# Norm totals in two rounded matmuls instead of one fp32 matmul, masks ahead of the scores, and 256 columns in the last mixer

## The chip, the cores and the metric

One core of one Trainium2 chip runs the whole program. The metric is device time in microseconds (us); the median of three runs before the change is 1474.05 us. TensorE does the matmuls, ScalarE the activations and copies that round, VectorE the elementwise work, GpSimd a share of it, and SyncE issues the loads.

## The reference

Two models run one after the other on 16 + 256 = 272 tokens of width 1024: a block with retention and forgetting attention, and then two layers, each of which is

```python
h = h + 0.5 * swiglu(rmsnorm(h, ffn1_norm[l]), ...)
h = h + hybrid_mixer_2(rmsnorm(h, mix_norm[l]), ...)
h = h + 0.5 * swiglu(rmsnorm(h, ffn2_norm[l]), ...)
# hybrid_mixer_2
q, k, v, a, b, g_sb, g_conv = split(u @ w_in)
y_sb = stick_breaking_attention(q, k, v) @ w_attn_out
y_conv = silu(layernorm(depthwise_conv31(a * sigmoid(b)))) @ w_conv_out
m = (sigmoid(g_sb) * y_sb + sigmoid(g_conv) * y_conv) @ w_out
```

Every norm divides by a root of a mean over the 1024 channels (512 in the layer norm), computed for each token. The channels lie on the partitions, so a sum over channels is a matmul with a matrix of ones. Only the last 256 tokens are returned.

## The kernel before

Activations are kept transposed: 128 channels on the partitions, tokens along the free dimension. A "slab" is a weight matrix of 1024 x 128 (eight 128 x 128 blocks); for each block TensorE runs three fp32r matmuls (high weight by high activation, high by low, low by high: lines 1509 to 1511 in `slab`, 1570 to 1572 in `first_pair`), 24 in all, into one of four PSUM banks `W[0..3]`. SyncE loads a slab to `raw`, ScalarE rounds it (`hi`, line 475), VectorE or GpSimd subtracts the rounded part (`lo_ahead`, line 904; `lo`, line 417). Each engine runs its own list of instructions in order; semaphores tie them. The weights of a slab go into one of four slots, and `hi_ahead` for the slab three places on stands in ScalarE's list at step `s` of the current one. TensorE may start slab `s` only when slab `s` - 3 has been taken out of its bank (`emptied`, `evac_done`).

**Norm statistics.** The squares of the 8 chunks of `h` are added into `acc` by VectorE (line 930). `stat(p)` is one fp32 matmul of `ones` by `acc`, placed inside `first_pair` (the first two slabs of the next stage, interleaved block by block) ahead of block `STAT_AT` = 5. ScalarE takes the root (line 483) and VectorE the reciprocal (line 910), which scales every slab of the stage as it leaves its bank (`scaled`, line 915). There are such totals for norms p = 1 to 7, and one more (`fin_acc`) of the first block's final norm, directly behind `first_pair` of the first layer.

**The mixer** runs 36 slabs, steps s = 0 to 35 of `for s in range(4 * N_MIX)`, on every engine. With `SB_FROM` = 14, `c, phase = divmod(s - 14, 4)`: TensorE runs `scores(c)` behind the slab of phase 0 (c = 0 to 3), `values(c - 1)` behind that of phase 1 (c = 1 to 4), `sums(c)` behind that of phase 3. ScalarE and VectorE do the softening between (`soften`, `keeps`, `round_keep`, `weights`). VectorE also runs the 31 taps of four channel groups (`taps`, line 1364) in those steps, up to s = 29. `LN_FROM` = 30: at s = 30 VectorE adds the four groups (`ln_sum`), TensorE sums over channels in fp32 behind slab 31 (`channel_sums(1)`), VectorE subtracts the mean at s = 32, ScalarE squares at s = 33, VectorE adds at s = 34, TensorE sums behind slab 35 (`channel_sums(2)`), then root, reciprocal, gain, Silu and rounding, while TensorE runs four double slabs of the attention branch; the convolution branch waits for `s_lo`.

In the second layer the first 16 tokens aren't needed past the keys and values; the query, gate and output slabs run on 256 columns there (`t` = 16), but the convolution, the layer norm and the attention's output still run on 272.

## Time and profile before

| what | value |
|---|---|
| median of 3 runs | 1474.05 us (1473.8 to 1474.22) |
| profiled execution | 1474.35 us, its span 1472.5 us |
| PE busy | 1465.1 us, 99% |
| DVE, ACT, POOL busy | 903.1, 769.0, 495.6 us |
| granted TensorE clock, mean | 0.999 |
| chain that ended last | PE 97%, POOL 1%, DVE 1% |
| DMA | mean 170 GB/s |

A share of busy time counts a matmul from its start to its modelled end, so matmuls in a row overlap; what a matmul costs in a row is the distance between two starts. An fp32 matmul is recorded as two instructions.

### The profile page before, as it was taken

To read this page: it belongs to the slowest core of one execution; us is meant where nothing else is said; L and a number is where in the kernel's file an instruction comes from. 1 tells how busy PE (TensorE), PEld (TensorE's weight loads), DVE (VectorE), ACT (ScalarE), POOL (GpSimd) and SP (SyncE) were. 2 spreads that over 40 slices of the span, in tenths; PEclk is the share of its full clock that TensorE was granted. 3 is DMA by queue.
4 is the path that set the end of the run, shared out by engine and by line. 5 is a ranking of instruction groups with operands and counts; after the bars stand their busy time and mean duration, and the time that the engine had idled before them with its cause. 6 is when DMAs were issued, how large, how long until landed. Compare 5 with 4: busy or idle time off the path is not lost.

```text
span 1472.5 us, 31298 instructions
## 1 busy us (share of the span) xinstructions
PE 1465.1 (99%) x11531; PEld 1430.3 (97%) x11531; DVE 903.1 (61%) x1568; ACT 769.0 (52%) x1087; POOL 495.6 (34%) x208
## 2 busy tenths in 40 slices
PE   9999999999999999999999999999999999999998
PEld 7999999989999999999999999999999999999987
DVE  6437888755445468998644434444437899854443
ACT  6446655545444446567544544444435557654443
POOL 5541000443334304710244433433420660044443
PEclk9999999999999999999999999999999999999999
DMA  7335566655556545445555654555644545566663
GB/s 265 120 100 168 171 189 192 216 162 161 174 176 210 164 129 164 146 146 164 173 174 177 201 182 134 173 176 187 200 149 139 163 142 171 165 195 185 207 201 107
DMA packets 65852, 250.97 MB, mean 170 GB/s; under 512 B 7280, under 2 KB 8688, under 8 KB 65776
## 3 DMA queue, kind: packets, MB, share of 16 engines
q1 hardware_dynamic: 65776, 249.92, 54.7%
q8 instruction: 53, 0.87, 0.2%
q14 instruction: 23, 0.19, 0.0%
HBM read 248.84 MB, written 1.05 MB: 170 GB/s over the span
## 4 chain that ended last, share of the span: by engine, by line
PE 97%; POOL 1%; DVE 1%; DMA 0%; issue 0%; ACT 0%; SPq 0%; DVEq 0%; POOLq 0%
PE W L1509 27%; PE W L1511 27%; PE W L1510 27%; PE W L1604 5%; PE XP L1629 3%; PE W L1603 3%; PE XQ L1629 2%; PE W L1570 1%; PE W L1571 1%; PE W L1572 1%; DMA raw<-in_w 0%; POOL wlo L417 0%; PE XQ L1549 0%; PE XQ L1728 0%; ACT whi L475 0%
## 5 line engine op out<-in xcount | busy, mean ns | idle before, releaser
L417 POOL TENSOR_TENSOR wlo<-raw,whi 128x1024 fp32r<-128x1024 f32 (+1 forms) x183 | 476.1, 2606 | 939.8 <-ACT whi L475 939.8
L1509 PE MATMUL W<-xh,whi 128*128 128x272 f32 (+2 forms) x2400 | 691.2, 288 | 0.2 <-POOL wlo L417 0.2
L1511 PE MATMUL W<-xh,wlo 128*128 128x272 f32 (+2 forms) x2400 | 686.7, 286 | 0.0
L1510 PE MATMUL W<-xl,whi 128*128 128x272 f32 (+2 forms) x2400 | 685.3, 286 | 0.0
L475 ACT ACTIVATE whi<-raw 128x1024 fp32r<-128x1024 f32 (+1 forms) x437 | 483.3, 1110 | 129.8 <-PE W L1511 101.6
L1509 PEld LDWEIGHTS W<-xh,whi 128*128 128x128 f32 x2400 | 452.1, 188 | 3.0 <-issue 1.9
L1511 PEld LDWEIGHTS W<-xh,wlo 128*128 128x128 f32 x2400 | 452.2, 188 | 0.0
L1510 PEld LDWEIGHTS W<-xl,whi 128*128 128x128 f32 x2400 | 451.9, 188 | 0.3
L904 DVE TENSOR_TENSOR wlo<-raw,whi 128x1024 fp32r<-128x1024 f32 (+1 forms) x253 | 330.9, 1308 | 60.2 <-ACT whi L475 60.0
L1509 PE MATMUL W<-ax,whi 128*128 128x272 f32 (+2 forms) x838 | 241.0, 288 | 0.1
L1511 PE MATMUL W<-ax,wlo 128*128 128x272 f32 (+2 forms) x838 | 240.5, 287 | 0.0
L1510 PE MATMUL W<-ax,whi 128*128 128x272 f32 (+2 forms) x838 | 240.4, 287 | 0.0
L1510 PEld LDWEIGHTS W<-ax,whi 128*128 128x128 f32 x838 | 158.9, 190 | 0.1
L1509 PEld LDWEIGHTS W<-ax,whi 128*128 128x128 f32 x838 | 157.6, 188 | 0.6 <-DVE ax L1446 0.3
L1511 PEld LDWEIGHTS W<-ax,wlo 128*128 128x128 f32 x838 | 157.5, 188 | 0.0
L915 DVE TENSOR_TENSOR scr<-W,rinv 128x272 f32<-128x272 f32 (+2 forms) x140 | 60.4, 431 | 117.8 <-PE W L1511 117.1
L518 ACT ACTIVATE ax<-W 128x272 f32 (+3 forms) x88 | 34.7, 395 | 182.8 <-DVE W L993 182.8
L1604 PE MATMUL W<-ax,whi 128*128 128x512 f32 x330 | 115.6, 395 | 0.0
L515 ACT ACTIVATE scr<-scr 128x272 f32<-128x272 f32 (+1 forms) x110 | 46.9, 426 | 107.0 <-DVE scr L915 75.7
L915 DVE TENSOR_TENSOR W<-W,rinv 128x272 f32<-128x272 f32 (+1 forms) x88 | 39.1, 444 | 96.1 <-PE W L1511 96.1
L1364 DVE SCALAR_TENSOR_TENSOR XQ<-scr,prm,XQ 128x272 f32<-128x272 f32 x184 | 92.9, 505 | 5.7
L1603 PE MATMUL W<-ax,wlo 128*128 128x256 f32 x330 | 92.4, 280 | 0.0
(262 smaller groups left out, 1221.5 us busy)
## 6 DMA issues: line engine op xcount, KB each, us to landing
raw<-in_w SPq DMA_DIRECT2D x358, 512.0 KB, 3.6
raw<-in_w SPq DMA_DIRECT2D x80, 704.0 KB, 4.1
h<-in_hT SPq DMA_DIRECT2D x4, 272.0 KB, 4.9
scr<-in_cst SPq DMA_DIRECT2D x1, 1000.0 KB, 9.8
out<-h SPq DMA_DIRECT2D x3, 256.0 KB, 2.4
raw<-in_w SPq DMA_DIRECT2D x2, 256.0 KB, 3.7
cst<-in_cst SPq DMA_DIRECT2D x1, 472.0 KB, 7.7
out<-h SPq DMA_DIRECT2D x2, 128.0 KB, 2.2
```

The costliest lines, as they stand in the source:

```text
L417: pool.tensor_tensor(wlo[:, j, 0:cols], raw[:, j, 0:cols], whi[:, j, 0:cols].bitcast(F32), ALU.subtract).then_inc(lo_ready[j], 1)
L475: act.activation(whi[:, j, 0:cols], raw[:, j, 0:cols], ACT.Copy).then_inc(hi_ready[j], 1)
L515: act.activation(actv[:, b, t:], gate[:, b, 2 + t:T + 2], ACT.Silu).then_inc(act_ready, 1)
L904: dve.tensor_tensor(wlo[:, slot, 0:cols], raw[:, slot, 0:cols], whi[:, slot, 0:cols].bitcast(F32), ALU.subtract).then_inc(lo_ready[slot], 1)
L915: return dve.tensor_tensor(out, W[bank][:, t:T], rinv[:, t:], ALU.mult)
L1364: ins = dve.scalar_tensor_tensor(total, u[:, c, k:k + T], w, total, ALU.mult, ALU.add)
L1509: pe.matmul(out, whi[:, j, w], mh, start=start and k == 0, stop=False, skip_group_check=True)
L1510: pe.matmul(out, whi[:, j, w], ml, start=False, stop=False, skip_group_check=True)
L1511: ins = pe.matmul(out, wlo[:, j, w], mh, start=False, stop=stop and k == len(rhs) - 1, skip_group_check=True)
L1603: pe.matmul(W[out][:, 0:T - T_B], wlo[:, j, w], ah[:, c, T_B:], start=c == 0, stop=False, skip_group_check=True)
L1604: ins = pe.matmul(both, whi[:, j, w], ax[:, c, :, T_B:], start=False, stop=c == FC - 1, skip_group_check=True)
L1629: return pe.matmul(out, lhsT, rhs, start=start, stop=True, skip_group_check=True)
```

## The change

1. `round_sum` (ScalarE) copies `acc` to `sum_r[:, 0]` in fp32r, `low_sum` (VectorE) subtracts that from `acc` into `sum_r[:, 1]`, and `stat` becomes two fp32r matmuls with `minus_r` (minus ones); the sign goes into the `scale` of the root. `stat` moves from ahead of block 5 to behind the whole first pair. The statistic of p = 0 and that of the last norm stay as they are.
2. The total of the final norm of the first block goes the same way, and moves behind slab 2 of its stage.
3. Both channel totals of each mixer go the same way. The rounding stands in ScalarE's list at s = 31 and s = 35 ahead of `hi_ahead`, the subtraction in VectorE's list at s = 31 and s = 35 ahead of the evacuation of that slab.
4. In `scores` the two mask matmuls (fp32r) go ahead of the twelve score matmuls; `values(c - 1)` moves from behind the slab of phase 1 to behind that of phase 0, directly behind `scores(c)`.
5. In the second layer the taps, the layer norm, its Silu and rounding, and the attention's values run on 256 columns.

```diff
+        sum_r = ax[:, FC - 1, :, :]
@@ ScalarE
             def sqrt_stat(p, t=0, fin=False):
                 act.wait_ge(stat_mm, p + 1)
-                act.activation(rinv[:, t:], X[3][:, t:T], ACT.Sqrt, scale=1.0 / D,
+                act.activation(rinv[:, t:], X[3][:, t:T], ACT.Sqrt, scale=-1.0 / D if p else 1.0 / D,
+            def round_sum(p, t=0, fin=False):
+                act.wait_ge(acc_done, 8 * p + 8)
+                if fin:
+                    act.wait_ge(meta_sum, 1)
+                act.activation(sum_r[:, 0, t:], acc[:, t:], ACT.Copy).then_inc(sum_hi, 1)
@@ ffn_up
+                round_sum(p, ta, fin)
                 hi_ahead(g, 0, own, own)
                 sqrt_stat(p, ta, fin)
+                if fin:
+                    act.wait_ge(fin_add, DC)
+                    act.activation(sum_r[:, 0, T_B:], fin_acc[:, T_B:], ACT.Copy).then_inc(fin_hi, 1)
@@ mixer
-                            act.activation(u[:, k, CONV_K - 1:], y[:, k, :], ACT.Square).then_inc(ln_sq, 1)
+                            act.activation(u[:, k, CONV_K - 1 + t:], y[:, k, t:], ACT.Square).then_inc(ln_sq, 1)
+                    if s == 0:
+                        round_sum(p - 1)
+                    if s in (LN_FROM + 1, LN_FROM + 5):
+                        k = s // (LN_FROM + 5) + 1
+                        act.wait_ge(ln_sum, 2 * l + k)
+                        act.activation(sum_r[:, 0, t:], acc[:, t:], ACT.Copy).then_inc(ln_high, 1)
                     hi_ahead(g + s // 4, s % 4, K8A, K8A)
@@ VectorE
+            def low_sum(p, t=0):
+                dve.wait_ge(sum_hi, p)
+                dve.tensor_tensor(sum_r[:, 1, t:], acc[:, t:], sum_r[:, 0, t:].bitcast(F32), ALU.subtract).then_inc(sum_lo, 1)
@@ ffn_up
+                low_sum(p, ta)
                 lo_ahead(g, 0, own, own)
                 norm_factor(p, ta)
+                if fin:
+                    dve.wait_ge(fin_hi, 1)
+                    dve.tensor_tensor(sum_r[:, 1, T_B:], fin_acc[:, T_B:], sum_r[:, 0, T_B:].bitcast(F32), ALU.subtract).then_inc(fin_lo, 1)
@@ mixer
+                    if s in (LN_FROM + 1, LN_FROM + 5):
+                        k = s // (LN_FROM + 5) + 1
+                        dve.wait_ge(ln_high, 2 * l + k)
+                        dve.tensor_tensor(sum_r[:, 1, t:], acc[:, t:], sum_r[:, 0, t:].bitcast(F32),
+                                          ALU.subtract).then_inc(ln_low, 1)
@@ TensorE
             def stat(p, t=0):
+                if p:
+                    if p == 1:
+                        pe.wait_ge(minus_ready, 1)
+                    pe.wait_ge(sum_lo, p)
+                    mm(X[3][:, t:T], minus_r[:, :], sum_r[:, 0, t:], True)
+                    mm(X[3][:, t:T], minus_r[:, :], sum_r[:, 1, t:], False).then_inc(stat_mm, 1)
+                    return
@@ first_pair
-                    if k == STAT_AT and norm is not None:
-                        stat(norm, t[0])
...
+                if norm is not None:
+                    stat(norm, t[0])
@@ scores
+                    for bank in range(2):
+                        own = X[bank][:, 0:SBW].rearrange("p (s n) -> p s n", n=SB_SEG)[:, 0:3:2, :]
+                        masks = hider[:, :].rearrange("p (s n) -> p s n", n=SB_SEG)[:, 0:3:2, :]
+                        mm(own, identr[:, :], masks, True)
@@ values
+                        skip = 0 if b else t
...
-                            ins = mm(X[2][p0:p0 + 64, P * b:T], vT[:, b, P * c + p0:P * c + p0 + 64],
-                                     attn[:, bank, SB_AT[b]:SB_AT[b] + T - P * b], b == 0)
+                            ins = mm(X[2][p0:p0 + 64, P * b + skip:T], vT[:, b, P * c + p0:P * c + p0 + 64],
+                                     attn[:, bank, SB_AT[b] + skip:SB_AT[b] + T - P * b], b == 0)
@@ channel_sums
-                    pe.wait_ge(ln_sum, 2 * l + k)
-                    mm(X[3][:, 0:T], ones, acc[:, :], True).then_inc(ln_mm, 1)
+                    pe.wait_ge(ln_low, 2 * l + k)
+                    mm(X[3][:, t:T], minus_r[:, :], sum_r[:, 0, t:], True)
+                    mm(X[3][:, t:T], minus_r[:, :], sum_r[:, 1, t:], False).then_inc(ln_mm, 1)
@@ mixer
-                    if phase == 1 and 1 <= c <= CC:
+                    if phase == 0 and 1 <= c <= CC:
                         values(c - 1)
```

## Rows read from the trace of the kernel before

**Rows 1.** The page's busy times of each engine.

```profile
PE 1465.1 (99%) x11531; PEld 1430.3 (97%) x11531; DVE 903.1 (61%) x1568; ACT 769.0 (52%) x1087; POOL 495.6 (34%) x208
```

**Rows 2.** Timeline of PE around `stat(3)`: start, length, instruction, count.

```profile
531.67 0.62 PE L1549 MATMUL XQ<-acc,cst 128*128 128x272 f32 x2
...
532.25 0.29 PE L1571 MATMUL W<-xl,whi 128*128 128x272 f32 x1
532.38 0.29 PE L1572 MATMUL W<-xh,wlo 128*128 128x272 f32 x1
```

**Rows 3.** Timeline of PE around `scores(0)` of the first layer.

```profile
575.15 0.29 PE L1511 MATMUL W<-xh,wlo 128*128 128x272 f32 x1
575.37 1.10 PE L1629 MATMUL XP<-proj,scr 64*128 64x272 f32 x12
...
576.77 0.29 PE L1509 MATMUL W<-xh,whi 128*128 128x272 f32 x1
```

**Rows 4.** Timeline of PE around `values(0)` of the first layer.

```profile
594.93 0.29 PE L1511 MATMUL W<-xh,wlo 128*128 128x272 f32 x1
595.15 1.00 PE L1629 MATMUL XQ<-scr,vT 128*64 128x272 f32 x12
...
596.31 0.29 PE L1510 MATMUL W<-xl,whi 128*128 128x272 f32 x1
```

**Rows 5.** Timeline of PE at the channel totals (first layer once, then second).

```profile
643.73 0.73 PE L1629 MATMUL XQ<-acc,cst 128*128 128x272 f32 x2
...
1209.40 0.94 PE L1629 MATMUL XP<-ax,later_r 128*128 128x432 f32 x4
...
1216.84 1.00 PE L1629 MATMUL XQ<-scr,vT 128*64 128x272 f32 x12
1217.88 0.72 PE L1629 MATMUL XQ<-acc,cst 128*128 128x272 f32 x2
...
1218.56 0.28 PE L1510 MATMUL W<-xl,whi 128*128 128x256 f32 x1
...
1229.77 0.62 PE L1629 MATMUL XQ<-acc,cst 128*128 128x272 f32 x2
...
1230.35 0.28 PE L1510 MATMUL W<-ax,whi 128*128 128x256 f32 x1
```

**Rows 6.** Timeline of DVE, first layer: evacuations of slabs 27, 28, 29 and 31.

```profile
628.02 0.44 DVE L915 TENSOR_TENSOR proj<-W,rinv 128x272 f32<-128x272 f32 x1
...
632.16 0.44 DVE L915 TENSOR_TENSOR proj<-W,rinv 128x272 f32<-128x272 f32 x1 [0.16 <-PE W L1511]
...
635.19 0.44 DVE L915 TENSOR_TENSOR proj<-W,rinv 128x272 f32<-128x272 f32 x1 [0.20 <-PE W L1511]
...
644.69 0.43 DVE L915 TENSOR_TENSOR proj<-W,rinv 128x272 f32<-128x272 f32 x1
```

**Rows 7.** Timeline of DVE, second layer: evacuations of slabs 27, 29 and 31.

```profile
1203.17 0.42 DVE L915 TENSOR_TENSOR proj<-W,rinv 128x256 f32<-128x256 f32 x1
...
1209.76 0.41 DVE L915 TENSOR_TENSOR proj<-W,rinv 128x256 f32<-128x256 f32 x1
...
1219.21 0.42 DVE L915 TENSOR_TENSOR proj<-W,rinv 128x256 f32<-128x256 f32 x1
```

**Rows 8.** Windows: PE, PEld, DVE, ACT, POOL busy, clock, DMA share, GB/s.

```profile
1214.17:1224.07 9.90, 9.86 (x86) 9.38 (x85) 9.65 (x20) 9.21 (x11) 0.00 (x0) 1.00 0.37 115
1224.71:1228.69 3.98, 3.98 (x36) 3.98 (x35) 3.92 (x7) 1.76 (x2) 0.00 (x0) 1.00 0.72 208
...
1469.00:1470.00 1.00, 0.00 (x0) 0.00 (x0) 0.48 (x2) 0.00 (x0) 0.00 (x0) 1.00 1.06 352
```

**Rows 9.** Timelines of ACT and DVE behind `stat(7)`, entry of the last FFN.

```profile
1282.66 2.01 ACT L475 ACTIVATE whi<-raw 128x1024 fp32r<-128x1024 f32 x2 [1.36 <-PE W L1572]
...
1287.21 0.41 DVE L915 TENSOR_TENSOR scr<-W,rinv 128x256 f32<-128x256 f32 x1
```

**Rows 10.** Timeline of PE at the start of the program: `keep_warm`.

```profile
1.46 4.00 PE L1629 MATMUL XP<-vT 128*128 128x272 f32 x8 [1.46 <-DVE vT L1137]
```

More of the change, by code:

```diff
@@ L297, in build @@
         wo_half, minus_ready = sem("wo_half"), sem("minus_ready")
+        sum_hi, sum_lo, fin_hi, fin_lo = (sem(x) for x in ("sum_hi", "sum_lo", "fin_hi", "fin_lo"))
+        ln_high, ln_low = sem("ln_high"), sem("ln_low")
         glu_sig, u_ready, conv_step = (sem(x) for x in ("glu_sig", "u_ready", "conv_step"))
@@ L816, in out_hi @@
                     act.wait_ge(o_mm, CC * l + c + 1)
-                    act.activation(ah[:, c, :], X[2][:, 0:T], ACT.Copy).then_inc(o_hi, 1)
+                    act.activation(ah[:, c, t:], X[2][:, t:T], ACT.Copy).then_inc(o_hi, 1)
                 ga = g + N_MIX
@@ L865, in mixer @@
                     act.wait_ge(ln_silu, CC * l + c + 1)
-                    act.activation(ah[:, CC + c, :], y[:, c, :], ACT.Copy).then_inc(s_hi, 1)
+                    act.activation(ah[:, CC + c, t:], y[:, c, t:], ACT.Copy).then_inc(s_hi, 1)
                 hi_ahead(ga, 3, K8D, K8D)
@@ L1344, in taps @@
                     for c, k, in_psum, before in TAPS[s]:
-                        total = X[3][:, 0:T]
+                        total = X[3][:, t:T]
                         if k is not None:
@@ L1357, in taps @@
                         if k is None:
-                            ins = dve.tensor_tensor(y[:, c, :], total, y[:, c, :], ALU.add)
+                            ins = dve.tensor_tensor(y[:, c, t:], total, y[:, c, t:], ALU.add)
                         elif not in_psum:
-                            ins = dve.scalar_tensor_tensor(y[:, c, :], u[:, c, k:k + T], w, y[:, c, :], ALU.mult, ALU.add)
+                            ins = dve.scalar_tensor_tensor(y[:, c, t:], u[:, c, k + t:k + T], w, y[:, c, t:], ALU.mult, ALU.add)
                         elif k == EARLY_TAPS + 1:
-                            ins = dve.tensor_scalar(total, u[:, c, k:k + T], w, None, ALU.mult)
+                            ins = dve.tensor_scalar(total, u[:, c, k + t:k + T], w, None, ALU.mult)
                         else:
-                            ins = dve.scalar_tensor_tensor(total, u[:, c, k:k + T], w, total, ALU.mult, ALU.add)
+                            ins = dve.scalar_tensor_tensor(total, u[:, c, k + t:k + T], w, total, ALU.mult, ALU.add)
                         ins.then_inc(conv_step, 1)
@@ L1383, in mixer @@
                         dve.wait_ge(conv_step, TAP_N * (l + 1))
-                        dve.tensor_tensor(acc[:, :], y[:, 0, :], y[:, 1, :], ALU.add).then_inc(ln_step, 1)
-                        dve.tensor_tensor(sq[:, 0, :], y[:, 2, :], y[:, 3, :], ALU.add).then_inc(ln_step, 1)
+                        dve.tensor_tensor(acc[:, t:], y[:, 0, t:], y[:, 1, t:], ALU.add).then_inc(ln_step, 1)
+                        dve.tensor_tensor(sq[:, 0, t:], y[:, 2, t:], y[:, 3, t:], ALU.add).then_inc(ln_step, 1)
@@ L1386, in mixer @@
                         dve.wait_ge(ln_step, 5 * l + 2)
-                        dve.tensor_tensor(acc[:, :], acc[:, :], sq[:, 0, :], ALU.add).then_inc(ln_sum, 1)
+                        dve.tensor_tensor(acc[:, t:], acc[:, t:], sq[:, 0, t:], ALU.add).then_inc(ln_sum, 1)
+                    if s in (LN_FROM + 1, LN_FROM + 5):
[3 more added lines that the diff above has]
+                                          ALU.subtract).then_inc(ln_low, 1)
@@ L1398, in mixer @@
                         dve.wait_ge(ln_step, 5 * l + 5)
-                        dve.tensor_tensor(acc[:, :], acc[:, :], sq[:, 0, :], ALU.add).then_inc(ln_sum, 1)
+                        dve.tensor_tensor(acc[:, t:], acc[:, t:], sq[:, 0, t:], ALU.add).then_inc(ln_sum, 1)
                     if s < G_GLU:
@@ L1434, in mixer @@
                 dve.wait_ge(ln_sqrt, l + 1)
-                dve.reciprocal(sq[:, 0, :], acc[:, :]).then_inc(ln_rcp, 1)
+                dve.reciprocal(sq[:, 0, t:], acc[:, t:]).then_inc(ln_rcp, 1)
                 attn_gate(0)
@@ L1438, in mixer @@
                 for c in range(CC):
[L1439 removed]
+                    dve.tensor_tensor(y[:, c, t:], y[:, c, t:], sq[:, 0, t:], ALU.mult).then_inc(ln_norm, 1)
                 lo_ahead(ga, 1, K8D, K8D)
@@ L1473, in layer @@
                 ffn_down(g + L_DNA, p, K8D, 0.5, fin=l == 0)
+                low_sum(p)
                 lo_ahead(g + L_MIX, 0, K8D, K8D)
@@ L1581, in ffn_up @@
                 if fin:
-                    pe.wait_ge(fin_add, DC)
-                    mm(X[2][:, T_B:T], ones, fin_acc[:, T_B:], True).then_inc(fin_mm, 1)
-                for j in range(2, 4):
+                    project(g, 2, x_rhs(ta), t=ta)
+                    pe.wait_ge(fin_lo, 1)
+                    mm(X[2][:, T_B:T], minus_r[:, :], sum_r[:, 0, T_B:], True)
+                    mm(X[2][:, T_B:T], minus_r[:, :], sum_r[:, 1, T_B:], False).then_inc(fin_mm, 1)
+                for j in range(3 if fin else 2, 4):
                     t = tb if j % 2 else ta
@@ L1885, in scores @@
                             p0 = 64 * bank
-                            mm(X[bank][:, SB_AT[b]:SB_AT[b] + w], kpad[p0:p0 + 64, c, a:a + P], proj[p0:p0 + 64, QQ + c, a:T], b == 0)
-                    for bank in range(2):
-                        own = X[bank][:, 0:SBW].rearrange("p (s n) -> p s n", n=SB_SEG)[:, 0:3:2, :]
-                        masks = hider[:, :].rearrange("p (s n) -> p s n", n=SB_SEG)[:, 0:3:2, :]
-                        ins = mm(own, identr[:, :], masks, False)
+                            ins = mm(X[bank][:, SB_AT[b]:SB_AT[b] + w], kpad[p0:p0 + 64, c, a:a + P], proj[p0:p0 + 64, QQ + c, a:T], False)
                     ins.then_inc(z_mm, 1)
```

22 lines of the change are left out of this document (10 added, 12 removed).

## The prediction

> **What bounds the kernel now.** I read four views in this order. The page's busy times first: TensorE is busy 1465.1 us of a span of 1472.5 us, VectorE 903.1, ScalarE 769.0 [rows 1]. So the time is the length of TensorE's own list; a change pays only if it shortens that list, and costs only if it makes TensorE wait. Second the timeline of TensorE, read by distances between starts, because busy lengths overlap. Third the timelines of VectorE and ScalarE at the same places, to see what TensorE would wait for. Last the windows, for the sum of a chain of operations. The reader is to see that around the edit the mixer is tight: VectorE idles 0.16 and 0.20 us in the 7.17 us from slab 27 to slab 29 of the first layer and nowhere else up to slab 31 [rows 6], and not at all in the second layer [rows 7].
>
> Two lengths serve throughout. A slab on 272 columns takes 3.03 us (the evacuations of slabs 28 and 29, both right behind TensorE, are 632.16 and 635.19 [rows 6]). A slab on 256 takes 2.83: from 1218.56 less one matmul of 0.12 to 1229.77 there are four [rows 5].
>
> **What TensorE's list saves.**
>
> *Norm totals.* `stat(3)` starts at 531.67; the second fp32r matmul behind it starts at 532.25 and the third at 532.38, so one such matmul is 0.13 and the fp32 total costs 532.25 - 531.67 - 0.13 = 0.45 [rows 2]. Two rounded ones cost 0.25. Saved 0.20, for p = 1 to 7 and the total of the final norm: 8 x 0.20 = 1.6. Adding a wait there costs TensorE nothing: `stat` now stands 18 matmuls (2.3 us) later, and what it waits for (a copy of about 0.4 and a subtraction of about 0.4, as every 272-column operation of VectorE in rows 6) starts with the last addition, which was complete before the old place.
>
> The Trainium skill ("FP8 and Floating Point Precision", TensorE Precision Notes) has true fp32 as four passes of the array. By four times 0.13 the total would be 0.52 and the saving 0.27 each, 0.5 more in all for the eight; the row has 0.45, and the sum goes by it.
>
> *Channel totals.* Alone, the one at 1229.77 costs 1230.35 - 1229.77 - 0.12 = 0.46 [rows 5], against 0.25 or 0.24: 0.22 each, 0.9 for four. In the second layer TensorE also stood 1217.88 - 1216.84 - 0.93 = 0.11 before the first one; that goes into the new wait below. Sum 1.0.
>
> *Masks first, values behind scores.* A step between kinds costs time. Going into the scores TensorE starts at 575.37, where the next fp32r matmul would have started at 575.15 + 0.13 = 575.28: 0.09. Scores and masks end at 576.77, so the pair costs 1.49 [rows 3]. `values` goes in with the same 0.09 and out with 0.10: 596.31 - 0.13 - 595.06 = 1.12 in all, of which 0.93 is work [rows 4]. Together 2.61. In the new order: masks 0.27, in 0.09, scores 1.03, values 0.93, out 0.10 = 2.42. Saved 0.19 for each group that has both, c = 1 to 3 in two layers: 6 x 0.19 = 1.1. The bounds are 0 (if going from 64-row tiles of the scores to 64-column tiles costs as much as a change of kind) and 1.1; I take 1.1, since the rows show the cost at changes between fp32 and fp32r. Masks first by itself saves nothing: the work is the same and the step out only moves.
>
> *256 columns* on TensorE touch one of three blocks of `values`, 16 columns of 432 in 0.93: 0.03 x 4 = 0.1. Elsewhere they shorten VectorE.
>
> Total saved: 1.6 + 1.0 + 1.1 + 0.1 = 3.8 us.
>
> **What the new waits cost.**
>
> *First channel total, first layer.* Before, it waited for `ln_sum` alone, and TensorE got there at 643.73 [rows 5] with the sum just ready. Now there is a copy on ScalarE and a subtraction on VectorE, and the subtraction stands in VectorE's list behind the evacuation of slab 30 and its low part: exactly where the evacuation of slab 31 started, 644.69 [rows 6]. It ends 0.43 later, TensorE starts about 0.05 behind that: 645.17. TensorE itself would arrive at 643.83 (0.10 for the step out of fp32, which the old total didn't pay here). That is 1.34 if VectorE runs as before. It doesn't: `values` no longer lies between slabs 27 and 28, so TensorE does slabs 28 and 29 in 6.06, while VectorE's work between the evacuations of slabs 27 and 29 is 7.17 - 0.16 - 0.20 = 6.81 [rows 6]. VectorE starts at slab 27's end in both orders (its list over a whole group is about 15.8 of 16.2 us), so it is now 0.75 late at slab 29, and all that follows up to the sum is a fixed list. Wait: 1.34 + 0.75 = 2.1 us.
>
> *The same, second layer.* TensorE from slab 29's end, 1209.40, arrives before at 1216.84 + 0.93 = 1217.77, so 8.37 later [rows 5], and 8.44 in the new order. VectorE between slabs 27 and 29 has 6.59 [rows 7], less nine shorter operations at 16 columns less (0.017 each, the 0.43 against 0.41 of rows 6 and 7) = 6.42, against 5.66 of TensorE: with the 0.2 from a slab's end to its evacuation it stands at 0.96 behind slab 29's end. From there to the subtraction 1219.21 - 1209.76 = 9.45 [rows 7], less 13 x 0.017 = 9.23, then 0.41 and 0.05: 10.65. Wait 10.65 - 8.44 = 2.2.
>
> What is late next: in ScalarE's list at s = 31 the rounding waits for the same sum ahead of `hi_ahead`. The high part of slab 34 and all behind it (table load, high part, `out_hi`, the sigmoid of eight gates, table load, squares, high part of slab 36) slide by 3.6 us. From the start of the first to the end of the last that list is 9.21 busy in the old trace [rows 8]. It starts behind the copy, 1.4 ahead of the total, so the high part of slab 36 is ready 7.8 to 7.9 behind the start of the total, its low part on VectorE 1.2 later; TensorE wants it after four slabs, 11.6 and more. Hidden. The load into that slot waits for the low part, not for the later high part, and slides by under 2 us of a 12 us turn. VectorE, however, has that low part ahead of the additions of the squares, and then three additions, an evacuation and another low part: 3.92 busy together [rows 8], then the subtraction, 0.4. That puts the second rounded total 7.9 + 3.9 + 0.4 + 0.05 = 12.3 behind the start of the first. TensorE arrives 0.25 + 4 x 3.03 = 12.4 behind in the first layer: no wait. In the second, 0.24 + 11.33 = 11.57 against 12.3 less shorter operations 0.3 = 12.0: 0.4. Waits at channel totals: 2.1 + 2.2 + 0.4 = 4.7.
>
> *Entry of each FFN.* The root now starts behind the pair and delays two high parts (2.01) that started at 1282.66, by 0.55 [rows 9]: 0.2 to 0.3 from the matmul to the root, 0.47 the root. VectorE's low part and the first evacuation, 1287.21, follow: done at 1288.17. TensorE wants the bank two slabs and two rounded matmuls behind the pair; the old pair ended 0.1 behind 1282.66, the new one 0.45 sooner: 1282.32 + 0.24 + 5.66 = 1288.22. It fits with 0.05 to spare in the last FFN and with 0.3 to 0.4 in those on 272 columns, where slabs are longer. I take 0.1 for the lot, with bounds 0 and 1.5. In the mixer's entry the root stood behind a high part that starts at the pair's end anyway, so the move doesn't lengthen it.
>
> Sum: -3.8 + 4.7 + 0.1 = **+1.0 us**. The profiled execution took 1474.35 us (span 1472.5, 1.85 around it), so its like would be 1475.35; the median of the runs is 0.3 below that execution, so **1475.0 us**.
>
> **The rivals.**
>
> A, *the forecast*: TensorE's list is shorter by about 3.8 and the totals wait about as much. Bounds: 1472.5 (VectorE isn't pushed by the move of `values`, -1.5, and the second total doesn't wait, and a little more saved) to 1477.3 (nothing saved by the merge, 1.1, and 1.2 at the FFN entries).
>
> B, *the waits are hidden*: 1474.05 - 3.8 = 1470.2. For it speaks that VectorE and ScalarE have 39% and 48% of the span free; against it the order of VectorE's list behind `ln_sum`, 1.8 us that nothing shortens.
>
> C, *other side, the FFN entries*: the first evacuation misses TensorE at four entries. Price 1 us each where POOL's and VectorE's low parts collide: 1475.0 + 4 = 1479. It decides from a root more than 0.4 later than I have it, on 272 columns. Against it: everything in that chain is in rows 9 with its length.
>
> D, *the clock*: a wait of 2.2 us lets TensorE fall from its level of 2.4 GHz to 1.2. At the program's start eight passes took 4.00, 0.50 each [rows 10], where two passes of a total later take 0.45 together [rows 2]; one slab at that rate is 3 us more. One such slab per layer: 1475.0 + 6 = 1481. Against it: with no matmul for some 3 us at the end of the program the granted clock still reads 1.00 in 1469 to 1470 [rows 8]. The Trainium skill ("TensorE: Matmul & The Clock Gate", Why this matters for your kernels) warns of gaps in the middle of a kernel that bring the clock back to half; by that rule waits of 2 us are near enough to count this case, and the row speaks for the full clock.
>
> E, *the change of type doesn't pay*: two rounded matmuls cost what one fp32 did. Then 12 x 0.2 = 2.4 is missing: 1477.4. Rows 2 speak against it.
>
> **How the numbers follow.** A 0.73, B 0.13, C 0.06, D 0.04, E 0.04. A measurement of this kernel can tell 0.2% (2.95 us) from no change: 1471.1 to 1477.0. Faster is B and a sliver of A, 0.14. Slower is C, D, E and 0.04 of A: 0.18. The same: 0.68. The likeliest case alone has 1472.5 to 1477.3; toward B the range reaches to 1471.3, toward C to 1477.6, which leaves out most of B, C and D, 2 in 10.
>
> **What the new profile would show.** Right: the total at s = 31 starts 10 to 11 us behind slab 29's end in both layers, with TensorE idle about 2 us before it, and ScalarE's high part of slab 34 directly behind the new copy. `stat` behind the first pair without idle time. `values` directly behind `scores`, the step between them under 0.05. The second total waits in the second layer only. PE busy less by about 4 us and its idle time more by 5. Wrong: if the idle before the totals is under 1 us, B; if TensorE waits for evacuation behind the third slab of an FFN, C; if matmuls behind the wait are 0.24 apart, D.

## The result, and the profile after

The changed kernel takes 1478.13 us (median of 10 runs, 1476.81 to 1479.79), the one before 1474.20 (10 runs, 1473.80 to 1474.41): ratio 1.0025, interval 1.0017 to 1.0033. It is slower by a quarter of a per cent, clear of the noise of both. The forecast was 1475.0 us, with 1477.6 as its upper end.

The profiled execution took 1476.81 us with a span of 1475.0, against a span of 1472.5 before: +2.5 us, where the sum of the prediction had +1.0. The median of the runs lies another 1.3 us above that execution; this second part has its own cause (the clock, below).

The page of the changed kernel, busy times of the engines and the chain that ended last:

```profile
PE 1461.2 (99%) x11531; PEld 1428.5 (97%) x11531; DVE 906.1 (61%) x1580; ACT 772.6 (52%) x1099; POOL 494.9 (34%) x208
...
PE 95%; DVE 3%; POOL 1%; DMA 0%; ACT 0%; issue 0%; SPq 0%; DVEq 0%; POOLq 0%
```

TensorE has the same number of matmuls and is busy 3.9 us less than in [rows 1], and the kernel is slower all the same: of the chain 3% is VectorE now. TensorE's longest waits in the changed kernel (instruction line, who released it, us in total, times, longest); two shorter ones, of 0.4 and 0.3 us, lie before 24 us:

```profile
PE XQ L1671 <- DVE ax L1420: 3.8, 2, 2.1
PE XQ L1671 <- DVE ax L1032: 1.5, 1, 1.5
PE XP L1671 <- DVE vT L1166: 1.5, 1, 1.5
PE W L1544 <- DVE wlo L924: 0.5, 1, 0.5
```

The third is the start of the program ([rows 10]), there before too. L1420 is the subtraction of the channel totals, L1032 that of the final norm's total, L924 a low part of weights.

TensorE's timeline, at the final norm's total, the first channel total of each layer and the second one of the second layer (the bracket is the idle time before the instruction):

```profile
333.99 0.41 PE L1671 MATMUL XQ<-ax,minus_r 128*128 128x272 f32 x2
334.23 0.29 PE L1544 MATMUL W<-xh,whi 128*128 128x272 f32 x1
...
337.13 0.29 PE L1546 MATMUL W<-xh,wlo 128*128 128x272 f32 x1
338.95 0.50 PE L1671 MATMUL XQ<-ax,minus_r 128*128 128x256 f32 x2 [1.53 <-DVE ax L1032]
...
644.47 0.29 PE L1546 MATMUL W<-xh,wlo 128*128 128x272 f32 x1
646.52 0.52 PE L1671 MATMUL XQ<-ax,minus_r 128*128 128x272 f32 x2 [1.76 <-DVE ax L1420]
646.88 0.28 PE L1544 MATMUL W<-xh,whi 128*128 128x272 f32 x1
...
1218.51 0.28 PE L1546 MATMUL W<-xh,wlo 128*128 128x256 f32 x1
1220.87 0.50 PE L1671 MATMUL XQ<-ax,minus_r 128*128 128x256 f32 x2 [2.08 <-DVE ax L1420]
1221.21 0.28 PE L1544 MATMUL W<-xh,whi 128*128 128x256 f32 x1
...
1232.45 0.28 PE L1546 MATMUL W<-xh,wlo 128*128 128x256 f32 x1
1232.71 0.50 PE L1671 MATMUL XQ<-ax,minus_r 128*128 128x256 f32 x2
```

Read by distances between starts, with 0.13 (0.12 on 256 columns) for the matmul before: the totals start 1.69, 1.92, 2.24 and 0.14 late. A pair that TensorE reaches in its stride costs 334.23 - 333.99 = 0.24; behind a wait, 1221.21 - 1220.87 = 0.34. Each wait costs 0.1 more than it lasts.

From one total to the next the whole difference can be placed. The starts of the norm totals of the changed kernel are taken back by the 18 matmuls that now stand ahead of them (2.15, 2.26 or 2.12 us on 258, 272 or 256 columns):

| stretch | before | after | difference | what it is made of |
|---|---|---|---|---|
| start to `stat(1)` | 143.68 | 143.61 | -0.1 | nothing |
| to `stat(2)` | 187.65 | 188.12 | +0.5 | low part 0.5 late and a restart, less one total |
| to `stat(3)` | 200.34 | 201.71 | +1.4 | final norm's total 1.69 late, restart 0.1, less two totals |
| to first channel total, first layer | 112.06 | 113.08 | +1.0 | 1.92 late, less one total and three merges |
| to the second | 12.67 | 12.46 | -0.2 | one total |
| to `stat(4)` | 52.44 | 52.29 | -0.2 | one total |
| `stat(4)` to `stat(6)` | 399.81 | 399.39 | -0.4 | two totals |
| to first channel total, second layer | 109.23 | 110.21 | +1.0 | 2.24 late instead of 0.11, less one total and three merges |
| to the second | 11.89 | 11.84 | 0.0 | 0.14 late, restart, less one total |
| to `stat(7)` | 50.43 | 50.08 | -0.4 | restart, less one total |
| to TensorE's last group | 185.99 | 185.86 | -0.1 | one total |

The sum is +2.5. A "restart" is the 0.1 us behind a late start, a "merge" the joining of `scores` and `values`.

Rows for the merge of `values` with `scores`, which answer to [rows 3, 4]:

```profile
591.75 0.29 PE L1546 MATMUL W<-xh,wlo 128*128 128x272 f32 x1
591.88 0.42 PE L1671 MATMUL XP<-hider,identr 128*128 128x288 f32 x2
592.23 1.10 PE L1671 MATMUL XP<-proj,scr 64*128 64x272 f32 x12
593.26 1.00 PE L1671 MATMUL XQ<-scr,vT 128*64 128x272 f32 x12
594.19 0.40 PE L1544 MATMUL W<-xh,whi 128*128 128x272 f32 x1
594.42 0.29 PE L1545 MATMUL W<-xl,whi 128*128 128x272 f32 x1
```

The three together cost 594.42 - 591.75 - 0.25 = 2.42, as forecast (2.61 before). From scores to values there is no step: 593.26 - 592.23 = 1.03, and in the kernel before the masks start just as long behind the scores (575.37 and 576.40).

Why the final norm's total was late: the timelines of DVE and POOL there.

```profile
334.95 1.85 DVE L930 RECIPROCAL rinv<-rinv 128x272 f32<-128x272 f32 x1 [1.98 <-ACT rinv L486]
336.72 2.18 DVE L1032 TENSOR_TENSOR ax<-scr,ax 128x256 fp32r<-128x256 f32 x1
...
336.25 2.37 POOL L420 TENSOR_TENSOR wlo<-raw,whi 128x1024 fp32r<-128x1024 f32 x1 [8.32 <-ACT whi L478]
```

The subtraction L1032 has 256 columns and should take 0.4. It took 2.18 and ended 0.3 behind GpSimd's low part (336.25 + 2.37 = 338.62), beside which it ran. That it also stands behind a reciprocal of 1.85 was in the code, but I had costed only its own length. Alone at that place it would have ended at 336.72 + 0.42 = 337.14, before TensorE was there (337.13 + 0.13 = 337.26): what made TensorE wait is the time beside GpSimd. The kernel before had the same thing at the same place, in a low part of VectorE, where it cost nothing (DVE, then POOL):

```profile
335.97 2.58 DVE L904 TENSOR_TENSOR wlo<-raw,whi 128x1024 fp32r<-128x1024 f32 x1 [1.61 <-ACT whi L475]
...
335.07 2.39 POOL L417 TENSOR_TENSOR wlo<-raw,whi 128x1024 fp32r<-128x1024 f32 x1 [7.55 <-ACT whi L475]
```

Alone that low part takes 1.21, as the next one in the changed kernel does:

```profile
338.82 1.21 DVE L924 TENSOR_TENSOR wlo<-raw,whi 128x1024 fp32r<-128x1024 f32 x1
```

### The profile page after: what moved, and what is told of

Same layout as the page of the kernel before. It is cut to its first block, busy times and chain, and to the rows that moved or that the text cites. A ratio compares the mean times of both kernels' runs of the same rounds, so it can differ in the third digit from the quotient of the medians.

```text
span 1475.0 us, 31325 instructions
## 1 busy us (share of the span) xinstructions
PE 1461.2 (99%) x11531; PEld 1428.5 (97%) x11531; DVE 906.1 (61%) x1580; ACT 772.6 (52%) x1099; POOL 494.9 (34%) x208
## 4 chain that ended last, share of the span: by engine, by line
PE 95%; DVE 3%; POOL 1%; DMA 0%; ACT 0%; issue 0%; SPq 0%; DVEq 0%; POOLq 0%
PE W L1544 26%; PE W L1545 26%; PE W L1546 26%; PE W L1646 5%; PE W L1645 3%; PE XP L1671 2%; PE XQ L1671 2%; PE W L1608 1%; PE W L1609 1%; DVE XQ L1393 1%; PE W L1610 1%; DMA raw<-in_w 0%; DVE wlo L924 0%; POOL wlo L420 0%; ACT whi L478 0%
## 5 line engine op out<-in xcount | busy, mean ns | idle before, releaser
L924 DVE TENSOR_TENSOR wlo<-raw,whi 128x1024 fp32r<-128x1024 f32 (+1 forms) x253 | 329.8, 1304 | 56.6 <-ACT whi L478 56.3
L1393 DVE SCALAR_TENSOR_TENSOR XQ<-scr,prm,XQ 128x272 f32<-128x272 f32 (+1 forms) x184 | 91.4, 497 | 5.7
```

Source lines behind the costliest of these rows:

```text
L924: dve.tensor_tensor(wlo[:, slot, 0:cols], raw[:, slot, 0:cols], whi[:, slot, 0:cols].bitcast(F32), ALU.subtract).then_inc(lo_ready[slot], 1)
L1393: ins = dve.scalar_tensor_tensor(total, u[:, c, k + t:k + T], w, total, ALU.mult, ALU.add)
```

## The experiments

Each kernel was timed in 10 or 11 runs against the one before on the same chip (1474.15 to 1474.39 there). For the spans, each of one profiled execution, the kernel before has 1472.5, the changed one 1475.0. Such a span carries some tenths that have nothing to do with an edit: `stat(1)`, which stands ahead of all that experiments 1 and 4 touch, starts at 145.76 in the changed kernel, at 146.05 in experiment 1 and at 145.32 in experiment 4.

**1. The final norm's rounding and subtraction ahead of the entry's weights and of the root**, into a buffer of their own.

```diff
+        fin_sr = ax[:, FC - 2, :, :]
@@ ScalarE, ffn_up
                 round_sum(p, ta, fin)
+                if fin:
+                    act.wait_ge(fin_add, DC)
+                    act.activation(fin_sr[:, 0, T_B:], fin_acc[:, T_B:], ACT.Copy).then_inc(fin_hi, 1)
                 hi_ahead(g, 0, own, own)
                 sqrt_stat(p, ta, fin)
-                if fin:
-                    act.wait_ge(fin_add, DC)
-                    act.activation(sum_r[:, 0, T_B:], fin_acc[:, T_B:], ACT.Copy).then_inc(fin_hi, 1)
@@ VectorE, ffn_up: the subtraction likewise, from behind norm_factor to behind low_sum
...
```

> Edit: the rounding and the subtraction of the total of the first block's final norm go ahead of the first high and low part of the FFN's entry, into a spare chunk; all else as in the changed kernel. Theory 1 (VectorE's subtraction stood behind the reciprocal and ran beside GpSimd's low part, 2.18 us instead of 0.42): it takes 0.42 now, the 1.5 us that TensorE waited for it and the 0.1 to 0.2 of the restart are gone, span 1473.3. Theory 2 (the entry is late because the root moved behind the pair): the wait only moves to the first evacuation, span 1474.6 or more. Theory 3 (waits let the clock fall in some executions, 1.3 us each time): with one wait less, fewer of the runs are slow, but some are, since two waits of 2 us remain.

Measured: span 1473.4, median 1476.29, ratio 1.0013 (1.0004 to 1.0023). The subtraction, in the timeline of DVE:

```profile
331.55 0.42 DVE L1031 TENSOR_TENSOR ax<-scr,ax 128x256 fp32r<-128x256 f32 x1
```

It takes 0.42 away from GpSimd's low part, TensorE doesn't wait there, and the span is 1.6 shorter, as theory 1 had it. That wait is settled. The clock falls in 7 of the 10 runs still (theory 3): two waits of about 2 us are left.

**2. Channel totals one slab later.** The first total behind slab 32, the mean at s = 33 and the squares at s = 34.

```diff
@@ TensorE, mixer; on VectorE and ScalarE likewise from LN_FROM + 2 to + 3 and from + 3 to + 4
-                    if s == LN_FROM + 1:
+                    if s == LN_FROM + 2:
                         channel_sums(1)
```

> Edit: the first channel total of each mixer stands behind slab 32 instead of 31, the subtraction of the mean at s = 33 and the squares at s = 34; all else as in the changed kernel. Theory 1 (VectorE's list behind the sum makes TensorE wait 1.9 to 2.3 us in each layer): both waits go, nothing takes their place, the second total doesn't wait, span 1475.0 - 4.1 = 1470.9. Theory 2 (the layer norm's chain has no room for a slab's delay): the second total or the convolution branch waits about as long, span 1474 to 1475. Theory 3 (clock): most runs at a mean clock of 0.999, few at 0.998.

Measured: span 1471.8, median 1473.89, ratio 0.9997 (0.9987 to 1.0006). TensorE's waits for L1420:

```profile
PE XQ L1671 <- DVE ax L1420: 1.5, 2, 1.2
```

The first totals no longer wait; 1.5 us come back at the second totals (0.35 and 1.2), so the result lies between the two theories, 0.9 above the first. The chain behind the first total has to be done in one slab less now; which part of it is late was not tried.

**3. Both moves, and the norm's total inside the first pair**, ahead of block 6 instead of behind the pair.

```diff
@@ first_pair, beside the edits of 1 and 2
+                    if k == 6 and norm is not None:
+                        stat(norm, t[0])
...
-                if norm is not None:
-                    stat(norm, t[0])
```

> Edit: both of the moves above, and the statistics back into the first pair, ahead of its block 6. If the waits at the two channel totals (4.1), at the final norm's total (1.7) and at the first FFN's entry (0.5) are all that went wrong, the span is 1475.0 - 6.3 = 1468.7, the time 1470.5, faster than before by 3.7 us, and every run shows a mean clock of 0.999. If the gains of the rounded totals were mis-sized as well, it lands between 1470.5 and 1474.

Measured: span 1469.7, median 1471.53 (1471.04 to 1471.88), ratio 0.9981 (0.9972 to 0.9990). TensorE's waits, but for the program's start:

```profile
PE XQ L1672 <- DVE ax L1421: 1.5, 2, 1.2
PE W L1545 <- POOL wlo L421: 0.3, 1, 0.3
```

The span is 1.0 above the 1468.7 of the expectation: the two waits at the second totals are those of experiment 2. What the change of type saves is read where nothing waits: from `stat(4)` to `stat(6)` it is 399.38 us, as in the changed kernel, against 399.81 before: 0.22 for each total.

**4. Idle matmuls ahead of the late totals.** The changed kernel with four fp32 matmuls on unused data ahead of each first channel total, and three ahead of the final norm's: the delay stays, the idleness goes.

```diff
                 def channel_sums(k):
+                    if k == 1:
+                        keep_warm(4)
@@ the final norm's total
+                    keep_warm(3)
                     pe.wait_ge(fin_lo, 1)
```

> Edit: the changed kernel, with idle matmuls on zeros put where TensorE waits: 4 fp32 ones (1.8 us) ahead of each mixer's first channel total, 3 (1.4 us) ahead of the final norm's total; their results are used by nobody. Theory 3 (a wait of about 2 us lets TensorE's clock fall in some executions, about 1.3 us each time): the profiled span stays at 1475.0 to 1475.3, and all runs lie within 0.5 us of each other at a mean clock of 0.999, median 1476.9. Theory 4 (the scatter of 1.3 us comes from elsewhere, loads for instance): runs still fall into two groups, and the median stays near 1478.

Measured: span 1474.4, median 1476.44, all of 11 runs in 1476.10 to 1477.17. The changed kernel's runs lie in three groups, 1476.81 to 1476.92 (mean granted clock 0.999), 1478.12 to 1478.50 (0.998) and one at 1479.79 (0.997). With the waits filled none of the lower clocks is left: that is theory 3, though the runs lie 1.1 us apart and not within 0.5. The median is 0.5 below the 1476.9 expected; 0.4 of it lies ahead of `stat(1)`.

**5. Only the order on TensorE**: the kernel before, with masks first and `values` behind `scores`, nothing else.

```diff
@@ scores: the masks ahead, as in the change
...
@@ mixer
-                    if phase == 1 and 1 <= c <= CC:
+                    if phase == 0 and 1 <= c <= CC:
                         values(c - 1)
```

> Edit: the kernel before, with the masks ahead of the scores and the values directly behind the next scores; all totals stay as single fp32 matmuls, all columns as before. Forecast's term: 0.19 us saved for each of six groups, and VectorE 0.75 us later at slab 29. If the merge saves what the rows say and the later VectorE makes the first channel total wait in its old form by 0.5 to 0.75 in each layer, the span is 1472.5 - 1.1 + 1.3 = 1472.7 (bounds 1472.0 to 1473.0). If the change of tiles from scores to values costs as much as a change of kind, nothing is saved and the span is 1473.8.

Measured: median 1474.49 (before 1474.15), ratio 1.0001 (0.9992 to 1.0011), span 1472.9. TensorE's wait beside the start:

```profile
PE XQ L1629 <- DVE acc L1387: 0.9, 1, 0.9
```

VectorE does get late against TensorE in the second layer, with the plain total, too. In the first layer there is no wait: in the kernel before the sum is complete at 643.29 there, 0.44 ahead of the total (643.73), where the prediction had it just ready, in the second layer at 1217.83, only 0.05 ahead (1217.88). With nothing waiting, the first layer also shows what the new order saves: from `stat(3)` to the first total 111.69 us against 112.06, 0.37 less. That is three merges at 0.19, less 0.19 for the last `values`, which now stand alone between fp32r slabs and no longer beside the fp32 total.

**6. Everything but the move of `values`**: the changed kernel with `values` behind the slab of phase 1 again.

```diff
-                    if phase == 0 and 1 <= c <= CC:
+                    if phase == 1 and 1 <= c <= CC:
                         values(c - 1)
```

> Edit: the changed kernel, with the values again behind the slab of phase 1; masks stay first, everything else stays. Theory 1 (moving the values pushed VectorE late at slab 29, in both layers, on top of its list behind the sum): the two waits of 1.8 and 2.1 us shrink by 0.5 to 0.75 each, the merge's 1.1 is lost, span 1475.0 - 1.3 + 1.1 = 1474.8, and no run shows a mean clock below 0.999 through these waits (the one of 1.5 at the final norm's total stays). Rival (the wait is VectorE's list behind the sum alone): the waits stay at 1.8 and 2.1, span 1476.1, clock as in the changed kernel.

Measured: span 1474.7, median 1476.48 (1475.97 to 1476.83), ratio 1.0016 (1.0006 to 1.0025). TensorE's waits for L1420:

```profile
PE XQ L1671 <- DVE ax L1420: 2.9, 2, 1.5
```

3.8 became 2.9 (1.38 and 1.51, where the changed kernel has 1.76 and 2.08), so the move of `values` put 0.4 and 0.6 on the two waits, not the 0.75 that I had for each. The span is that of theory 1 (1474.8). And the move earns nothing here: from `stat(3)` to the first channel total the changed kernel, with the move, takes 0.03 us longer than this one (110.82 against 110.79), from `stat(6)` to that of the second layer 0.20 (107.95 against 107.75). What it saves went into the wait.

**7. The second total's subtraction earlier as well**: kernel 3, with that subtraction at s = 34 ahead of the low part.

```diff
-                    if s in (LN_FROM + 1, LN_FROM + 5):
+                    if s == LN_FROM + 1:
...
+                    if s == LN_FROM + 4:
+                        dve.wait_ge(ln_high, 2 * l + 2)
+                        dve.tensor_tensor(sum_r[:, 1, t:], acc[:, t:], ...)
```

> Edit: the version with the three moves, and the subtraction of the second channel total's low part at s = 34 ahead of VectorE's low part of weights instead of at s = 35 behind it. The waits there were 0.35 and 1.2 us; VectorE's low part is 1.13. Theory 1: the first goes, the second shrinks to 0.1 or less, the restart's 0.1 goes with the first, span 1469.7 - 1.5 = 1468.2, time 1470.0, the best so far. Theory 2 (the rounding on ScalarE is what is late): both stay, span 1469.7.

Measured: median 1471.55, ratio 0.9982 (0.9973 to 0.9991), span 1469.8: no change from kernel 3, where theory 1 had 1.5 us less. The timeline of PE:

```profile
1226.65 0.51 PE L1675 MATMUL XQ<-ax,minus_r 128*128 128x256 f32 x2 [0.29 <-DVE ax L1449]
...
1239.32 0.39 PE L1548 MATMUL W<-ax,whi 128*128 128x256 f32 x1 [0.41 <-DVE ax L1484]
```

The waits at the second totals do shrink (none, and 0.29), so theory 2 is out as well. Counted from the first total the second one starts 0.90 sooner than in kernel 3 (9.20 against 10.10), but `stat(7)` comes 0.27 later (60.93 against 60.66). In between TensorE is late at the double slabs behind it, at 1235.80 by 0.19, at 1239.32 by 0.58 and at 1251.02 by 0.19, with a restart each time; in kernel 3 it is in time at the first two. In the first layer one such place (667.13, 0.30 late) takes 0.4 of the 0.5 won. The view of waits lists only the largest of these. The wait was moved, not removed: what comes behind the second total has four double slabs of cover, and those begin sooner as well. Which operation sets its end was not tried.

**8. One idle stretch filled, not the other**: `keep_warm(4)` in the second layer alone.

```diff
+                    if k == 1 and l == 1:
+                        keep_warm(4)
```

> Edit: the changed kernel, with four idle fp32 matmuls (1.8 us) only ahead of the second layer's first channel total, the longest wait (2.1); the waits of 1.8 in the first layer and 1.5 at the final norm's total stay empty. If the wait of 2.1 alone let the clock fall, all runs are at 0.999 and within 0.5 us. If the first layer's does it too, some runs still lie 1.3 us higher, but none 2.6 higher.

Measured: median 1477.32; six of 11 runs at 1476.62 to 1477.32 (clock 0.999 to 1.0), five at 1477.82 to 1478.35 (0.998), none at 0.997. The profiled execution is one of the five, and shows the fall behind the first layer's wait (us, then PE, PEld, DVE, ACT, POOL busy, granted clock, DMA share, GB/s):

```profile
646.00:648.00 2.00, 1.62 (x8) 1.62 (x9) 2.00 (x4) 1.99 (x2) 0.00 (x0) 0.65 0.41 88
648.00:650.00 2.00, 2.00 (x11) 2.00 (x11) 1.65 (x5) 2.00 (x3) 0.00 (x0) 0.50 0.75 236
```

So the first layer's wait of 1.8 lets the clock fall by itself, and the third group, missing in 11 runs here, is the one with both falls (experiment 9).

**9. The norm's total inside the first pair, alone**, the rest as in the changed kernel.

```diff
+                    if k == 6 and norm is not None:
+                        stat(norm, t[0])
...
-                if norm is not None:
-                    stat(norm, t[0])
```

> The changed kernel with one edit: the norm's total stands inside the first pair, ahead of its block 6, instead of behind the pair. Theory 1: the first FFN entry misses its low part by 0.5 us only because the root, and with it two high parts, starts later than in the kernel before. With the total 12 matmuls (1.5 us) sooner that wait goes, with 0.1 of restart, and nothing else does: span 1475.0 - 0.6 = 1474.4, the wait of 1.5 at the final norm's total is still there, since its subtraction still runs beside GpSimd's low part. Theory 2 (rival): the whole list behind the root moves up 1.5 us at that entry too, so that the subtraction of the final norm's total no longer runs beside GpSimd's low part, takes 0.4 instead of 2.2, and that wait goes as well: span 1474.4 - 1.8 = 1472.6. The subtraction stands behind the reciprocal in both.

Measured: median 1475.87 (1473.85 to 1477.31), ratio 1.0009 (1.0000 to 1.0018). The runs in full: 1473.85, 1474.03, 1474.56, 1474.60 (0.999); 1475.74, 1475.87, 1476.16, 1476.26 (0.998); 1477.28, 1477.29, 1477.31 (0.997). The first four have spans of 1472.1 to 1472.8, as theory 2 has it. DVE and POOL at the final norm's total:

```profile
332.54 1.85 DVE L930 RECIPROCAL rinv<-rinv 128x272 f32<-128x272 f32 x1 [0.49 <-ACT rinv L486]
334.31 0.36 DVE L1032 TENSOR_TENSOR ax<-scr,ax 128x256 fp32r<-128x256 f32 x1
...
334.36 2.56 POOL L420 TENSOR_TENSOR wlo<-raw,whi 128x1024 fp32r<-128x1024 f32 x1 [7.36 <-ACT whi L478]
```

The subtraction started 0.05 ahead of GpSimd's low part and took 0.36, right behind the reciprocal in both kernels. Between 0.36 and 2.18 lies only which of the two comes first.

This kernel's profiled execution fell into the lowest group, and shows what the clock does. Windows around the first totals of both layers:

```profile
644.00:646.00 2.00, 1.96 (x9) 1.96 (x10) 1.97 (x4) 1.99 (x3) 0.00 (x0) 0.55 0.50 141
646.00:648.00 2.00, 2.00 (x12) 2.00 (x12) 1.35 (x4) 2.00 (x2) 0.00 (x0) 0.60 0.62 188
648.00:650.00 2.00, 2.00 (x18) 2.00 (x17) 0.86 (x2) 1.97 (x4) 0.00 (x0) 1.00 0.54 203
...
1218.00:1220.00 2.00, 0.08 (x1) 0.08 (x1) 2.00 (x5) 1.88 (x3) 0.00 (x0) 1.00 0.00 0
1220.00:1222.00 2.00, 2.00 (x14) 2.00 (x15) 1.97 (x4) 1.99 (x3) 0.00 (x0) 0.76 0.57 150
1222.00:1224.00 2.00, 2.00 (x11) 2.00 (x11) 1.14 (x4) 1.98 (x3) 0.00 (x0) 0.50 0.83 197
```

And its PE timeline behind the first of them:

```profile
644.04 0.72 PE L1671 MATMUL XQ<-ax,minus_r 128*128 128x272 f32 x2 [1.76 <-DVE ax L1420]
644.56 0.43 PE L1544 MATMUL W<-xh,whi 128*128 128x272 f32 x1
...
647.51 0.33 PE L1545 MATMUL W<-xl,whi 128*128 128x272 f32 x1
```

Behind each wait the granted clock stands at 0.5 for a stretch, the level of 1.2 GHz. From 644.56 to 647.51 there are 13 matmuls at 0.227 instead of 0.126: 1.3 us, and the pair costs 0.52 where it cost 0.36 in the changed kernel: 0.2. That makes 1.5, about the distance between the groups (their medians lie 1.7 and 1.3 apart).

**10. The channel totals plain again**: kernel 3 with one fp32 matmul for each channel total at its old place, without the rounding and the subtraction. All norm totals stay rounded.

```diff
-                    pe.wait_ge(ln_low, 2 * l + k)
-                    mm(X[3][:, t:T], minus_r[:, :], sum_r[:, 0, t:], True)
-                    mm(X[3][:, t:T], minus_r[:, :], sum_r[:, 1, t:], False).then_inc(ln_mm, 1)
+                    pe.wait_ge(ln_sum, 2 * l + k)
+                    mm(X[3][:, t:T], ones, acc[:, t:], True).then_inc(ln_mm, 1)
```

> The kernel with the three moves, but its channel totals (layer norm) are one fp32 matmul each again, at their old places (behind slabs 31 and 35), without the rounding and the subtraction; all norm totals stay rounded. Theory 1: rounding the channel totals doesn't pay at any place tried: it saves 0.22 each, 0.9, and the second totals wait 0.35 and 1.2 for it, while a plain total there waits for nothing and the first one waits at most 0.9, in the second layer. 1471.5 + 0.9 - 1.5 + (0.3 to 0.9) = 1471.2 to 1471.8, no difference from 1471.53 that a measurement can tell, with fewer instructions. Theory 2 (rival): it pays its 0.9, since the chain of the layer norm is given back at the convolution branch anyway: 1472.4 or more.

Measured: median 1471.16 (1471.10 to 1471.58), ratio 0.9980 (0.9971 to 0.9989), span 1469.8. All of TensorE's waits:

```profile
PE XP L1663 <- DVE vT L1163: 1.5, 1, 1.5
PE XQ L1663 <- DVE acc L1413: 0.3, 1, 0.3
```

The rounded channel totals earn nothing that could be measured, at the best place found for them: theory 1. The sum closes within 0.3, too: eight norm totals at 0.22, six merges at 0.20 and 0.1 of columns make 3.1, less a wait of 0.3 is 2.8, where the span is 2.7 shorter and the median 3.1. The medians of kernels 3 and 7 are 2.9 and 2.6 below that of before; three kernels 0.4 us apart are hardly told from each other, and this one has the fewest instructions.

## Why the prediction was wrong

**What held.** The savings: forecast 3.8. The lateness and restarts of the table add up to 6.9, the span grew by 2.5, so TensorE's list is 4.4 shorter; 3.9 of it can be placed (12 totals at 0.22, forecast 0.20 to 0.22; six merges at 0.20, forecast 0.19; 0.1 of columns). Of the other 0.5, 0.27 lies in the second layer's last stretch: before, TensorE's convolution branch stood behind VectorE's rounding of its input, which ended at 1240.35 + 1.48 = 1241.83,

```profile
1240.35 1.48 DVE L1446 TENSOR_TENSOR ax<-scr,ax 128x272 fp32r<-128x272 f32 x4
```

and TensorE started at 1241.89 instead of 1241.62. In the changed kernel that chain runs on 256 columns and ends 0.4 sooner, counted from the second total, and the matmul at that place (1244.46) is in time. The prediction had let those shorter operations count for nothing on TensorE behind the totals. The rest is spread over the stretches. The waits at the channel totals: forecast 2.1, 2.2 and 0.4, measured 1.92, 2.24 and 0.14, at the places and behind the instruction named. Rival E is out: the type pays. So is B: two totals wait about 2 us each.

**Two steps failed, and the range holds with either one mended.** One is the sentence "Adding a wait there costs TensorE nothing", the other the dismissal of rival D, the clock. With the wait of the first taken away the median is 1476.29 (experiment 1), with the clock kept up 1476.44 (experiment 4); the changed kernel, with both, has 1478.13, above the range's end of 1477.6.

**"Adding a wait there costs TensorE nothing".** I wrote it for the norm totals and the final norm's total together, from a copy of 0.4 and a subtraction of 0.4. For the final norm's it is wrong by 1.69 + 0.1 us, which is more than the whole difference of 1.5 between forecast and measured span. What the sum counted on, that the copy and the subtraction start with the last addition, is so for the norm totals, whose operations stand at the front of the lists; none of them waits. Those of the final norm's total stand behind the root and behind `norm_factor`, which wait for the pair's total, and the subtraction then runs beside GpSimd's low part. Experiments 1 and 9 take it away in two ways (0.42, 0.36) and the wait goes both times. The rule I should have weighed is in the Trainium skill ("SBUF — State Buffer", SBUF: two separate sides): a VectorE operation with two SBUF inputs and a GpSimd operation that reads SBUF take a shared pair of ports for a whole instruction, and the one that comes second stands still until the first is done. The trace agrees, by 2.18 us against 0.36.

**The first FFN entry** cost 0.6 (a low part 0.5 late by the view of waits, and its restart), where I had 0.1 for all entries. I had followed the root up to the first evacuation, which was in time; what came late was the low part of a later slab, released at 158.02:

```profile
158.02 0.35 PE L1544 MATMUL W<-xh,whi 128*128 128x258 f32 x1 [0.47 <-DVE wlo L924]
```

With the total 1.5 us sooner (experiment 9) it is gone. So rival C's place was half right and its price too high; its other entries never missed.

**Sizes.** Forecast of the span's change +1.0, measured +2.5. The 1.5 between are: final norm's total +1.8, first entry +0.5, restarts at three channel totals +0.3, less 0.4 for waits forecast too long at the channel totals, less 0.6 to 0.7 for the shorter list. In the waits at the first channel totals the part for `values` was 0.75 and measured 0.4 and 0.6 (experiment 6); the part of VectorE's list behind the sum was 1.34 in the first layer, where experiment 6 has a wait of 1.38.

**The clock: rival D, at 0.04.** It was real. I had argued from the program's end, where no matmul ran for 3 us and the granted clock still read 1.00 [rows 8]. The row was read one window too early. The next one of the same trace, still without a matmul, has the fall:

```profile
1470.00:1472.50 2.50, 0.00 (x0) 0.00 (x0) 0.00 (x0) 0.00 (x0) 0.00 (x0) 0.62 0.62 216
```

So a clock of 1.00 in an idle stretch says nothing of what comes next; in experiment 9 too it reads 1.00 during the idle stretch (1218 to 1220) and falls behind it. The price was too high, 1.3 to 1.5 us for each fall instead of 3. It came from the passes of 0.50 at the program's start [rows 10], where the granted clock reads 1.00 from 2 to 4 us, so that no row shows that they are a matter of the clock; the rate behind a fall, 0.227 for a matmul instead of 0.126, is about half all the same. Nor did the low level hold as long as a slab takes at that rate: in experiment 9 it held from 644.0 to 647.6, in which half the work was still done. And it comes only in some executions, 6 of 10 of the changed kernel's. That adds 1.3 to its median, and is why the median stands 3.9 above that of before and not 2.5. The kernels whose longest wait behind the program's start is 1.5 or less (experiments 2, 3, 5, 6, 7, 10) show no run of a lower group, nor does the one with filled waits; those with 1.8 and 2.1 do (the changed kernel, experiments 1 and 9), and experiment 8 with the one of 1.8 alone. The Trainium skill ("TensorE: Matmul & The Clock Gate", Why this matters for your kernels) warns of gaps between matmuls in mid-kernel, but of longer ones; by it these waits would not count, and the measured falls behind 1.8 and 2.1 us decide otherwise. Why one execution has the fall and the next has not, no run here shows.

**What stays open.** Which operation of the layer norm's chain holds the second totals by 0.35 and 1.2 in experiment 3 was not tried one by one. In experiment 9 the subtraction came ahead of GpSimd's low part by 0.05 us in the profiled execution; that it does so in all the others is only what their spans, 1472.1 to 1472.8 in the runs without a fall, suggest.

## What to carry to other kernels

Making a matmul cheaper by splitting its input puts a copy and a subtraction ahead of it on two other engines. When TensorE arrives with the sum just ready, as at both layer norms here (0.44 and 0.05 us before it), 0.22 us of saving buys 2 us of waiting; when the sum is ready long before, as at the norm totals, it is profit (0.22 each), provided that the new operations go to the front of their lists. Of the kernels tried, the one that keeps the rounded norm totals in this way, and the channel totals plain, is 3.1 us faster than before (experiment 10). Cost a new operation on VectorE by where it stands in its list and by what GpSimd does at that moment, not by its own length, and look behind every wait of a microsecond or two for a lower granted clock, over several executions.

## What the runs showed of the hardware

- A two-input subtraction of 256 columns takes 0.36 to 0.42 us alone and 2.18 when GpSimd's low part started before it; it then ends 0.3 behind that operation. Started 0.05 ahead of it, it isn't delayed. A low part of 1024 columns takes 1.21 alone and 2.58 beside GpSimd's.
- A wait of 1.8 or 2.1 us of TensorE brings the granted clock to 0.5 behind it in a part of the executions, at 1.3 to 1.5 us each; one of 1.5 us never did here (six kernels, 63 runs). At the program's end it fell with no matmul running, in the window from 1470.0 to 1472.5 (0.62), where the one before it read 1.00.
- A restart behind a wait costs 0.1 us beside the wait, at full clock (a pair of 0.34 instead of 0.24).
- From matmuls on 64 rows to matmuls on 64 columns, both fp32, there is no step (1.03 us for twelve, to the start of the next); between fp32 and fp32r there is one of 0.09 to 0.10.
